# Handing TensorE a recurrence chunk in pieces between the k steps of a dense product, in one layer of a convolution and mLSTM encoder

## The reference, cut to what matters

```python
p = h @ w_in
bg, cg, xin, q, k, v, o, ip, fp = jnp.split(p, offs, axis=-1)
u = cg * xin                       # (A) gated width-3 causal convolution
y = conv_b + conv_w[0] * u_pad[:, :-2] + conv_w[1] * u_pad[:, 1:-1] + conv_w[2] * u_pad[:, 2:]
a_out = rmsnorm per group of (bg * y)
# (B) matrix memory with a state, chunk after chunk
s = einsum(q, k) * exp(d_log - m_t)             # decayed scores within the chunk
num = s @ v + w_inter * (q @ C)                 # C is the state carried between chunks
h = num / maximum(abs(den), exp(-m_t))
C_new = decay * C + k.T @ (wk * v)
hm = rmsnorm(h) * sigmoid(o)
x = x + concat(a_out, hm) @ w_out
```

## Time and profile before

| what | us |
|---|---|
| median of three runs | 2128.5 |
| lowest and highest run | 2125.5 and 2134.36 |
| profiled execution, first to last instruction | 2134.3 |
| the profiled execution's own time (the highest of the three) | 2134.36 |
| TensorE busy in it | 2053.9 (96%) |
| VectorE, ScalarE, GpSimd busy in it | 949.9, 515.4, 106.9 |
| mean granted TensorE clock, as a share of 2.4 GHz | 0.972 |

### The profile page before, as it was taken

One profiled execution on the slowest core, in us unless ns is written; L12 is line 12 of the kernel. 1 busy time (PEld: TensorE's weight loads), 2 busy tenths in 40 slices (PEclk: granted clock), 3 DMA queues, 4 the chain that ended last, 5 costly groups with the idle time before them and its releaser, 6 DMA issues. The chain is left out here.

```text
span 2134.3 us, 31347 instructions
## 1 busy us (share of the span) xinstructions
PE 2053.9 (96%) x12605; PEld 2022.3 (95%) x12605; DVE 949.9 (45%) x1598; ACT 515.4 (24%) x908; POOL 106.9 (5%) x141
## 2 busy tenths in 40 slices
PE   6799999999999998999999889999999999999996
PEld 5799999999999998999999879999999999999996
DVE  6633323432333348412666655633333433343247
ACT  4311111111111125322333331412112211112123
POOL 2100000000000012000000011100000000000012
PEclk8899999999999999998999989999999999999998
DMA  6011011110111011311110240121011101111002
GB/s 200 1 60 59 20 39 59 59 53 23 43 59 59 10 63 40 82 40 30 31 30 29 102 94 21 40 60 60 20 39 59 59 20 39 59 59 59 0 1 82
DMA packets 144037, 104.60 MB, mean 49 GB/s; under 512 B 6361, under 2 KB 136233, under 8 KB 143977
## 3 DMA queue, kind: packets, MB, share of 16 engines
q1 hardware_dynamic: 143976, 103.77, 16.0%
HBM read 94.83 MB, written 8.92 MB: 49 GB/s over the span
## 5 line engine op out<-in xcount | busy, mean ns | idle before, releaser
L219 PE MATMUL bank<-in_hi,w_hi 128*128 128x352 f32 x2256 | 744.5, 330 | 22.2 <-DVE in_lo L166 11.8
L225 PE MATMUL bank<-in_hi,w_lo 128*128 128x352 f32 x2256 | 733.1, 325 | 0.0
L224 PE MATMUL bank<-in_lo,w_hi 128*128 128x352 f32 x2256 | 731.6, 324 | 0.0
L219 PEld LDWEIGHTS bank<-in_hi,w_hi 128*128 128x128 f32 x2256 | 430.0, 191 | 28.5 <-issue 10.1
L224 PEld LDWEIGHTS bank<-in_lo,w_hi 128*128 128x128 f32 x2256 | 432.2, 192 | 1.3
L225 PEld LDWEIGHTS bank<-in_hi,w_lo 128*128 128x128 f32 x2256 | 430.0, 191 | 0.0
L394 DVE TENSOR_TENSOR ffn_hidden<-ffn_silu,bank 128x352 f32<-128x352 f32 x132 | 68.8, 521 | 658.0 <-PE bank L225 581.2
L219 PE MATMUL bank<-ffn_hidden_hi,ffn_w_hi_more 128*128 128x352 f32 x1056 | 343.7, 325 | 13.0 <-issue 11.9
L405 DVE SCALAR_TENSOR_TENSOR x<-bank,x 128x352 f32<-128x352 f32 x528 | 267.5, 525 | 167.5 <-PE bank L225 114.8
L225 PE MATMUL bank<-ffn_hidden_hi,ffn_w_lo_more 128*128 128x352 f32 x924 | 298.3, 323 | 0.0
L224 PE MATMUL bank<-ffn_hidden_lo,ffn_w_hi_more 128*128 128x352 f32 x924 | 298.0, 323 | 0.0
(11 more groups left out here) (196 smaller groups left out, 1623.0 us busy)
## 6 DMA issues: line engine op xcount, KB each, us to landing
raw<-in_ffn_w_gate SPq DMA_DIRECT2D x44, 512.0 KB, 4.0
ffn_raw_more<-in_ffn_w_down SPq DMA_DIRECT2D x44, 512.0 KB, 5.6
raw<-in_w_in SPq DMA_DIRECT2D x24, 512.0 KB, 3.9
raw<-in_ffn_w_up SPq DMA_DIRECT2D x22, 512.0 KB, 5.0
ffn_raw_more<-in_ffn_w_up SPq DMA_DIRECT2D x22, 512.0 KB, 5.5
x_parked<-x SPq DMA_DIRECT2D x3, 1408.0 KB, 5.6
x<-x_parked SPq DMA_DIRECT2D x3, 1408.0 KB, 11.0
raw<-in_w_out SPq DMA_DIRECT2D x8, 512.0 KB, 3.8
```

The lines of the kernel that those rows point to most:

```text
L219: pe.matmul(out, w_hi, in_hi, start=first, stop=False)
L224: pe.matmul(out, w_hi, in_lo, start=False, stop=False)
L225: return pe.matmul(out, w_lo, in_hi, start=False, stop=last)
```

## The change: pieces between k steps

The three stages and the columns of group 0 become generators that yield after each piece, and `product` takes one of them and draws one piece after each k step. `stage_a` is six pieces (v; k and the row; logs of two heads, twice; scores of two heads, twice), `stage_b` six (four heads, two state matmuls), `stage_c` yields once before its one piece. Each stage moves from behind a product into a product, with the waits that it had: in the channel tile stage a of even goes into cg block 0, stage c of the group before into cg block 1, stage b of even into cg block 2, stage a of odd into xin block 1, stage c of even into xin block 2 and stage b of odd into bg block 0. For group 0, the columns go into tile 10 block 0, stage a into tile 10 block 2 and stage b into tile 11 block 1. No instruction is added or taken away on any engine, no program but TensorE's is touched.

```diff
-            def product(b, j, bank=None):
+            def product(b, j, bank=None, between=()):
+                between = iter(between)
                 for k in range(KT):
                     ...
-                last.then_inc(s.dense_done, 1)
+                    if k == KT - 1:
+                        last.then_inc(s.dense_done, 1)
+                    next(between, None)
+                for _ in between:
+                    pass
...
-            pe.wait_ge(s.row_exp, 6)
-            pe.wait_ge(s.row_step, ROW_STEPS)
-            for g in range(GROUPS):
+            def columns():
+                pe.wait_ge(s.row_exp, 6)
+                pe.wait_ge(s.row_step, ROW_STEPS)
+                for g in range(GROUPS):
                     ...
+                        if (g * KINDS_COL + kind) % 4 == 3:
+                            yield
...
             def stage_a(g, t0, n):
                 ...
                 last.then_inc(s.v_turned, 1)
+                yield
                 ...
                 last.then_inc(s.k_turned, 1)
+                yield
                 ...
-                last.then_inc(s.logs_done, 1)
+                    if h == HEADS - 1:
+                        last.then_inc(s.logs_done, 1)
+                    if h % 2:
+                        yield
                 ...
-                last.then_inc(s.scores_done, 1)
+                    if h == HEADS - 1:
+                        last.then_inc(s.scores_done, 1)
+                    if h % 2:
+                        yield
...
             def stage_b(g, n, state):
                 ...
                     pe.matmul(out, queries[:, h, 0:n], state[:, h // 2, :], start=False, stop=True)
+                    yield
                 ...
-                last.then_inc(s.nums_done, 1)
+                    if p == 1:
+                        last.then_inc(s.nums_done, 1)
+                    yield
...
             def stage_c(g, n):
+                yield
                 turn_back(pe, g, n)
...
-                cg(0)
-                stage_a(even, c * (2 * CHUNK), CHUNK)
-                cg(1)
+                cg(0, stage_a(even, c * (2 * CHUNK), CHUNK))
                 if first:
-                    stage_c(0, DEC_SEQ)
+                    cg(1, stage_c(0, DEC_SEQ))
                 else:
-                    stage_c(c * 2, CHUNK)
-                cg(2)
-                stage_b(even, CHUNK, state_p)
+                    cg(1, stage_c(c * 2, CHUNK))
+                cg(2, stage_b(even, CHUNK, state_p))
                 pe.wait_ge(m.w_low, c * 3 + (QKVO_TILES + 3))
                 xin(0)
-                stage_a(odd, c * (2 * CHUNK) + CHUNK, CHUNK)
-                xin(1)
-                xin(2)
-                stage_c(even, CHUNK)
+                xin(1, stage_a(odd, c * (2 * CHUNK) + CHUNK, CHUNK))
+                xin(2, stage_c(even, CHUNK))
                 pe.wait_ge(m.w_low, c * 3 + (QKVO_TILES + 4))
-                bg(0)
-                stage_b(odd, CHUNK, state_p)
+                bg(0, stage_b(odd, CHUNK, state_p))
...
-            pe.wait_ge(s.state_in, 16 * 2 * HEADS)
-            stage_a(0, SEQ, DEC_SEQ)
-            qkvo_tile(QKVO_TILES - 2, 1)
-            stage_b(0, DEC_SEQ, state_s)
-            qkvo_tile(QKVO_TILES - 1, 2)
+            def sample_a():
+                pe.wait_ge(s.columns_ready, 2)
+                pe.wait_ge(s.constants, 7)
+                pe.wait_ge(s.state_in, 16 * 2 * HEADS)
+                yield from stage_a(0, SEQ, DEC_SEQ)
+
+            qkvo_tile(QKVO_TILES - 2, 1, (columns(), (), sample_a()))
+            qkvo_tile(QKVO_TILES - 1, 2, ((), stage_b(0, DEC_SEQ, state_s), ()))
```

More of the change, by code:

```diff
@@ L1629, in _, with qkvo_tile @@
                 product(b, 1, first_banks[1][b])
-            def qkvo_tile(n, j):
+            def qkvo_tile(n, j, between=((), (), ())):
                 pe.wait_ge(m.w_low, n + 2)
@@ L1634, in qkvo_tile @@
                     pe.wait_ge(s.qkvo_copied, n * 3 + (b - 2))
-                    product(b, j)
+                    product(b, j, between=between[b])
             qkvo_tile(2, 2)
@@ L1642, in _ @@
             qkvo_tile(QKVO_TILES - 3, 0)
-            pe.wait_ge(s.row_exp, 6)
-            pe.wait_ge(s.row_step, ROW_STEPS)
-            for g in range(GROUPS):
[L1647 to L1657, removed]
+            def columns():
+                pe.wait_ge(s.row_exp, 6)
+                pe.wait_ge(s.row_step, ROW_STEPS)
+                for g in range(GROUPS):
+                    t0, n = (SEQ, DEC_SEQ) if g == 0 else ((g - 1) * CHUNK, CHUNK)
+                    for kind, r in enumerate((ROW_A, ROW_WK, ROW_ENM)):
+                        at = (g * KINDS_COL + kind) * HEADS
+                        pe.transpose(num_bank[0:n, at:at + HEADS], rows[0:HEADS, r, t0:t0 + n],
+                                     sh.ident[0:HEADS, 0:HEADS])
+                        if (g * KINDS_COL + kind) % 4 == 3:
+                            yield
+                for p in range(PAIRS):
+                    last = pe.matmul(score_bank[:, p * GROUPS:(p + 1) * GROUPS], sh.pair_rows[:, p, :], decay_row[:, :],
+                                     start=True, stop=True)
+                last.then_inc(s.columns_done, 1)
             def stage_a(g, t0, n):
@@ L1707, in conv_tile, with cg @@
                 even, odd = c * 2 + 1, c * 2 + 2
-                def cg(b):
+                def cg(b, between=()):
                     if first:
@@ L1713, in cg, with xin, bg @@
                         pe.wait_ge(s.group_mean, c * 3 + (b - 2))
-                    product(b, 0)
-                def xin(b):
+                    product(b, 0, between=between)
+                def xin(b, between=()):
                     pe.wait_ge(s.cg_copied, c * 3 + (b + 1))
-                    product(b, 1)
-                def bg(b):
+                    product(b, 1, between=between)
+                def bg(b, between=()):
                     pe.wait_ge(s.u_made, c * 3 + (b + 1))
-                    product(b, 2)
+                    product(b, 2, between=between)
                 def stats(b):
```

## The result

The changed kernel takes 2148.49 us, the median of four runs (2147.21 to 2149.89), against 2127.0 us for the kernel before in the same comparison: a ratio of 1.009 with a 95% interval of [1.0072, 1.0109]; the medians alone stand at 1.010. By the medians it is slower by 21.5 us where 3.2 us were forecast, and lies 2.5 us outside the range. The profiled execution spans 2148.1 us.

A forecast was written before the change was run, and what follows sets the result against it. TensorE, 96% busy, loses time to clock dips and waits in the mixer. Costs of 21.2 us less gains of 18.0 us (3.0 waits, 15 clock) make it 3.2 us slower: 2137.6 us, range 2118 to 2146.

The forecast's parts named there:

- (a): Stage a of odd: TensorE newly waits for the state of even, 1.8 to 2.1 us per tile, together 7.8 us.
- (b): Stage b of odd: TensorE newly waits for the mixing of even, 1.35 or 1.75 us per tile, together 6.2 us.
- (c): Stage b of even in tile 0: TensorE newly waits for the mixing of group 0, 2.4 us, once.
- (d): cg block 0 of tile 0: TensorE newly waits for the copy of tile 11 block 0, 1.8 us, once.
- (2): Clock gain in the mixer: mixing pieces with products returns three quarters of the half-clock loss, 15 us.
- The base of 20 us: Time lost to the clock in the mixer's ten half-clock stretches: 20 us, with 12.5 and 22.1 us as bounds.
- The first rival: Stage a among k steps is too thin to hold the clock; 2146.7 us with nothing back; chance 0.24.
- The mixed stretch is nearer to stage b in what TensorE streams: Reason for expecting 15 us of clock back in mixed stage a: stretches of stage b stay at full clock.
- Term (e): Switches between four-row pieces or columns and 128-row products: 0.2 us each, 3 us over all, between 0 and 5.
- The sign set down for the clock: Between 957 and 1222 us: eight or more half-clock stretches staying would show the clock share wrong; two or three expected.
- The forecast of the tiles: Channel tiles 0 and 3 take 0 to 3 us longer, tiles 1 and 2 are shorter by about 1 us.

The follow-up runs named there:

- e2: The changed kernel with stage a and the columns back whole at their old places, only stages b and c in pieces: 2154.57 us, 1.013.
- e7: The changed kernel with stage b of odd whole behind bg block 0 again: 2142.53 us, 1.0062.
- e8: The changed kernel with 128 rows, filled up with zeros, instead of 4 in stage a's spreading matmuls: 2125.99 us, 0.9988.
- e0: The kernel before, profiled once more with no edit: 2125.36 us.
- e4: The kernel before, stages whole, with stage a's spreading matmuls on 128 rows filled up with zeros instead of 4: 2109.93 us, 0.9901.
- e5: e1 with the spreading matmuls of stage a on 128 rows instead of 4: 2106.35 us, 0.9883.
- e6: e1 with stage a's pieces reordered to v, logs, k, scores, logs, scores, four rows as before: 2118.57 us, 0.994.
- e9: e4 with only the columns and stage a of group 0 in pieces: 2107.78 us, 0.991.
- e1: The changed kernel with stages b and c whole behind their products again, only stage a and the columns in pieces: 2130.19 us, 1.0014.
- e3: The changed kernel with each stage in one go behind its product's first k step, not in pieces: 2141.14 us, 1.0072.

## Why the prediction was wrong

**The waits were right.** (a) was set at 7.8 us and measured 7.3; (b) and (c) together at 8.6 and measured 8.4; (d) at 1.8 and measured 1.8. e2, e7 and e8 show them again, each at its own size, and that a wait taken away does not come back at the next one. With the waits of before taken off and the statistics a little less late, waiting grew by 14.3 us where 15.2 had been worked out.

**The step that failed is (2), "I take three quarters, 15 us".** Next to nothing of the clock came back. The changed kernel's profile has 27.2 us at half clock in the part, e0 has 23.8; over the whole span the mean is 96 us for the four executions of the changed kernel and 99 us for the thirteen of the kernel before (89 to 111 us for single ones), so some 2 us of time were given back, if any. The base of 20 us was a little high, since it came from the slowest execution: the kernels whose falls are all or nearly gone (e4, e5, e6, e8, e9) have 27 to 36 us less at half clock in the mean than the kernel before beside them, so 14 to 18 us were to be had. e0's 23.8 us alone would say 12 us, which is too few. So the failure is in the share, not in the base.

The first rival had the reason right, that the stretch is too thin around the logs. e1 shows it with hardly a wait, e6 by moving only the order of the pieces. "The mixed stretch is nearer to stage b in what TensorE streams" was the wrong reading: e4 shows that stage b differs from stage a not in the products near it but in its 128 active rows, and whatever comes with them. Whether the new waits add to the falls is open. The first fall of the changed kernel stands among pieces of stage b with 128 rows, 1.1 us behind a wait of 2.5 us, and speaks for it, as do e2 and e3 at the same place; e7 and e8 have the same wait and no fall behind it. Where a fall comes also differs between two executions of one program (eight of eight stages and five of eight), and no run takes apart what decides that.

**Term (e) was mis-sized.** 3 us were taken, with 5 as the upper bound. e1 has as much time at half clock as e0 and 6.1 us more busy time, from stage a and the columns; e8 adds 3.1 us, together 9.2 us. I had drawn the term from the turn back, whose border with a product is free; it is a border between two sets of 128 rows. With four-row matmuls in it, a prompt's stage a in pieces takes 4.73 us of its own in e6 and 4.27 us whole, 0.46 us more where I took 0.2; a piece of columns costs 0.29 us where I took 0.2. The stages b were put at nothing: that is right for the prompt's, and short by 1.2 us for group 0's and by the 0.16 us that each new wait adds to busy time.

The sum made anew, with the mean clock: 14.3 us of waits and 9.2 us of busy time, less 2 us of clock, are 21.5 us, as the medians have it. So close a fit is luck, since each clock is known to 0.001, some 2 us of time. Of the 18.3 us missed, the clock accounts for 13 and the borders for 6, while the waits came out 0.9 us smaller than worked out. The chance of 0.24 for that rival was too low: every stage a of the profile was followed by a fall, and no row showed a mixed stretch that held. Whether transposes count for the clock is not settled here; e4 keeps its clock with a row of them opening each stage.

The sign set down for the clock did not warn of this. It was eight or more half-clock stretches, and there are four, but they are longer: the time at half clock says it, not the number of stretches.

The forecast of the tiles failed with it: tile 1 was to be shorter by a microsecond and is longer by 2.1, tile 0 was to be longer by at most 3 and is longer by 5.4.

## What to carry to other kernels

Before an instruction stream goes into the middle of a product, list what the product's last semaphore releases and what the product covered until now; both move by the whole length, and chains read from a trace of before gave the new waits here to within half a microsecond in sum. Cutting in pieces cost where a piece brought another number of active rows than the product: 0.46 us for a stage a with four-row matmuls, 0.02 us for the same stage with 128 rows. If small matmuls let the clock fall, first fill their rows with zeros: here that was worth some 20 us, half of it from the clock, without moving anything. And one profile is not enough to size a clock loss that changes from execution to execution.

## What the runs showed of the hardware that I had not expected

Matmuls with four active rows cost more than the same with 128: 0.57 us against 0.33 for a head's three records, next to 128-row neighbours. A whole prompt stage a with four-row matmuls was followed by half clock in eight of eight cases in one execution and five of eight in the other, the same stage with zeros in 124 more rows in none of eight. Cut in pieces with four active rows, it fell in five of eight cases in one order of the pieces and in none in another. The kernel before has 23.8 or 44.3 us at half clock in two executions of the same program, 10.8 us of span apart.
